# Turning the query and key sets of the mix on VectorE and through DRAM instead of on TensorE

## The reference, cut to what matters

```python
aq, ak, av, bq, bk, bv, cq, ck, cv, cg, gates = split(h @ w_in[l], ...)
qa = rope(rms(aq) * a_q_norm)       # 4 heads x 2 maps x 64
ka = rope(rms(ak) * a_k_norm)
y_a = diff_attention(qa, ka, va, lam, lam_init, a_subln)      # softmax map 1 - lam * softmax map 2
y_b = chunk_attention(rms(bq)*b_q_norm, rms(bk)*b_k_norm, vb, rel_bias)     # 8 heads x 64
y_c = retention(rope(cq), rope(ck) / 8, vc, cg, out_norm)     # 4 heads x 64, decay in place of softmax
x = x + (sum over a, b, c of sigmoid(gates) * (y @ w_branch)) @ w_out
```

## Time and profile before

| | |
|---|---|
| time, median of 3 runs | 1818.6 us (1818.33 to 1820.05) |
| span of the profiled execution, first to last instruction | 1816.7 us |
| the median less this span | 1.9 us |
| busy share: TensorE, its weight loads, VectorE, ScalarE, GpSimd | 99%, 82%, 52%, 50%, 75% |
| granted TensorE clock, mean | 0.999 of full speed |
| DMA | 366.61 MB, 202 GB/s over the span |

### The profile page before, as it was taken

One profiled execution on the slowest core, in us unless ns is written; L12 is line 12 of the kernel. 1 busy time (PEld: TensorE's weight loads), 2 busy tenths in 40 slices (PEclk: granted clock), 3 DMA queues, 4 the chain that ended last, 5 costly groups with the idle time before them and its releaser, 6 DMA issues.

```text
span 1816.7 us, 25068 instructions
## 1 busy us (share of the span) xinstructions
PE 1797.5 (99%) x9322; PEld 1482.3 (82%) x9322; DVE 942.8 (52%) x1756; ACT 905.1 (50%) x1337; POOL 1365.0 (75%) x568
## 2 busy tenths in 40 slices
PE   6999999999999999999999999999999999999999
PEld 5888888887889888887888888888888878888887
DVE  4673766678655524776553230714095865143152
ACT  3334424764456644455554644464445565545442
POOL 2624544559868898987689798969897858888885
PEclk9999999999999999999999999999999999999999
DMA  9853885748775775565466566567655645656653
GB/s 366 299 201 93 278 301 164 196 157 301 245 279 188 221 216 194 172 209 165 132 187 195 175 195 195 193 184 232 195 195 181 186 139 163 194 160 211 190 194 128
DMA packets 200697, 366.61 MB, mean 202 GB/s; under 512 B 32868, under 2 KB 54356, under 8 KB 200020
## 3 DMA queue, kind: packets, MB, share of 16 engines
q1 hardware_dynamic: 197568, 357.39, 61.6%
q10 hardware_dynamic: 3028, 7.86, 1.1%
HBM read 364.12 MB, written 6.13 MB: 204 GB/s over the span
## 4 chain that ended last, share of the span: by engine, by line
PE 98%; DMA 0%; ACTq 0%; ACT 0%; DVE 0%; POOL 0%; issue 0%; DVEq 0%
PE ps L1258 26%; PE ps L1260 26%; PE ps L1259 26%; PE ps L1384 3%; PE ps L1385 3%; PE ps L1386 3%; PE ps L1949 1%; PE ps L1951 1%; PE ps L1950 1%; PE ps L1306 1%; PE ps L1876 1%; PE ps L1655 1%; PE ps L1626 1%; PE ps L1636 1%; PE ps L1516 1%; PE ps L1921 1%
## 5 line engine op out<-in xcount | busy, mean ns | idle before, releaser
L616 POOL TENSOR_TENSOR w_lo<-raw,w_hi 128x1024 fp32r<-128x1024 f32 x556 | 1346.0, 2458 | 403.4 <-ACT w_hi L654 382.2
L1258 PE MATMUL ps<-w_hi,act_rows_r 128*128 128x512 f32 x2064 | 814.8, 395 | 3.2 <-POOL w_lo L616 3.1
L1260 PE MATMUL ps<-w_hi,act_rows_r 128*128 128x512 f32 x2064 | 804.8, 390 | 0.0
L1259 PE MATMUL ps<-w_lo,act_rows_r 128*128 128x512 f32 x2064 | 804.5, 390 | 0.0
L654 ACT ACTIVATE w_hi<-raw 128x1024 fp32r<-128x1024 f32 x556 | 571.1, 1058 | 359.4 <-DMA raw<-in_ffn_w_up 96.5
L1258 PEld LDWEIGHTS ps<-w_hi,act_rows_r 128*128 128x128 f32 x2064 | 387.9, 188 | 89.9 <-issue 8.6
L1260 PEld LDWEIGHTS ps<-w_hi,act_rows_r 128*128 128x128 f32 x2064 | 387.8, 188 | 81.8
L1259 PEld LDWEIGHTS ps<-w_lo,act_rows_r 128*128 128x128 f32 x2064 | 388.1, 188 | 77.2
L2604 DVE STREAM_TRANSPOSE ps<-proj 32x256 f32<-32x256 f32 (+1 forms) x384 | 166.6, 434 | 6.5
L2585 DVE TENSOR_TENSOR proj<-proj,ps 128x1024 f32<-128x1024 f32 (+1 forms) x18 | 20.4, 1132 | 252.2 <-PE ps L1260 247.8
L1384 PE MATMUL ps<-act_rows_r,w_hi 128*128 128x512 f32 (+1 forms) x288 | 101.4, 352 | 0.0
(11 more groups left out here) (245 smaller groups left out, 1559.9 us busy)
## 6 DMA issues: line engine op xcount, KB each, us to landing
raw<-in_w_in SPq DMA_DIRECT2D x120, 512.0 KB, 3.8
raw<-in_ffn_w_gate SPq DMA_DIRECT2D x88, 512.0 KB, 4.3
raw<-in_ffn_w_up SPq DMA_DIRECT2D x88, 512.0 KB, 4.3
raw<-in_ffn_w_down SPq DMA_DIRECT2D x88, 512.0 KB, 3.4
proj<-in_ada_w SPq DMA_DIRECT2D x39, 512.0 KB, 7.8
pt<-in_ada_w SPq DMA_DIRECT2D x38, 512.0 KB, 6.4
raw<-in_pool_w_in SPq DMA_DIRECT2D x32, 512.0 KB, 7.4
raw<-in_na_w_in SPq DMA_DIRECT2D x32, 512.0 KB, 5.4
```

The costliest lines, as they stand in the source:

```text
L616: pool.tensor_tensor(w_lo[:, s, :], raw[:, s, :], w_hi[:, s, :].bitcast(F32), ALU.subtract).then_inc(lo_done, 1)
L1258: pe.matmul(o, h, hi, start=start, stop=False)
L1259: pe.matmul(o, h, lo, start=False, stop=False)
L1260: return pe.matmul(o, c, hi, start=False, stop=stop)
```

## The change

All five sets (AK, AQ, BK, BQ, and CQ with CK) take one way. `set_squared` lets VectorE turn 32 x 32 squares in place of the partition quarter, with two transposes of 128 partitions x 512, one for each 128 tokens, into a staging area of 1024 columns in `proj`. This leaves features on partitions, but only within a quarter: what belongs to partition quarter k lies in the free range k of all four quarters. `keep_set` stores the staging area to a DRAM tensor (`set_rows`, 512 KB, two of them in turn), and `place_set` loads it back in four DMAs, one for each partition quarter, with runs of 1 KB. Both stand in the SyncE queue, behind the sends of block at + 8 and at + 9 of the mix, `at` being the third number in `MIX_SETS`. The staging area is free for the next set when the store has landed.

In `qt` a key set of branch A or B lies in runs of 32 tokens. A query set, and all of the C set, is interleaved: token p of a chunk and tile is at 8 p plus a small offset. So TensorE's stationary operand in every `scores` has a step of 8 words (32 bytes), its moving operand has runs of 32 words for units 0 to 7 and a step of 8 words for units 8 and 9. The number of products, their sizes and their order stay.

The factor 1/8 of AQ moves into the root of the head norms, the gains of BQ into one VectorE multiplication of 128 x 1024 (`queries_scaled`, after block 23, before `maps_joined(3)`). The outputs of branch A and B swap their chunks in `MIX_Y`. The TensorE transposes and the copies from PSUM go, with their waits.

```diff
-MIX_TURNS = ((AK, 4), (AK + 256, 6), (AQ, 0), (AQ + 256, 2), (BK, 12), (BK + 256, 14), (BQ, 8), (BQ + 256, 10), (CK, 18), (CQ, 16))
-MIX_TURN_AT = {13: (2, 3), 19: (6, 7), 31: (8, 9)}
+MIX_SETS = ((AK, 4, 7), (AQ, 0, 10), (BK, 12, 13), (BQ, 8, 18), (CQ, 16, 29))
+            def keep_set(l, q):
+                n = len(MIX_SETS) * l + q
+                sp.wait_ge(dve_done, dve_s.count(("set", l, q)))
+                if n >= 2:
+                    set_landed(sp, l if q >= 2 else l - 1, q - 2 if q >= 2 else q + len(MIX_SETS) - 2)
+                sp.dma_start(set_rows[n % 2], set_blocks([[1, 1024]])).then_inc(sets_kept, 16)
+            def place_set(l, q):
+                n = len(MIX_SETS) * l + q
+                sp.wait_ge(sets_kept, 16 * (n + 1))
+                for kq in range(4):
+                    src = bass.AP(set_rows.tensor, n % 2 * P * 1024 + 256 * kq, [[1024, 32], [32 * 1024, 4], [1, 256]])
+                    sp.dma_start(free(qt[32 * kq:32 * kq + 32, MIX_SETS[q][1], 0:1], [[256, 4], [1, 256]]), src).then_inc(sets_in[n % 2], 16)
...
+                            for q, (_, _, at) in enumerate(MIX_SETS):
+                                if g == at + SLOTS:
+                                    keep_set(layer, q)
+                                if g == at + SLOTS + 1:
+                                    place_set(layer, q)
...
+        def still_heads(chunk, rows, t):
+            base = chunk // 4 * 4
+            return free(qt[rows, base, 0:1], [[8, P]], 2 * (chunk - base) + t)
+        def moving_heads(chunk, rows, t, n):
+            return free(qt[rows, base, 0:1], [[32, n], [256, 4], [1, 32]], 32 * (2 * (chunk - base) + t))
+        def moving_between(chunk, rows, t, n):
+            return free(qt[rows, base, 0:1], [[1, n], [8, P]], 2 * (chunk - base) + t)
...
-                    for k in MIX_TURN_AT.get(G, ()):
-                        turn_heads(k)
...
+                def set_squared(q):
+                    if len(MIX_SETS) * l + q:
+                        dve.wait_ge(sets_kept, 16 * (len(MIX_SETS) * l + q))
+                    for t in range(NT):
+                        rows = free(proj[:, 0:1], [[P, 4], [32, 4], [1, 32]], MIX_SETS[q][0] + t * IN_COLS)
+                        if q in (SET_AK, SET_BK):
+                            last = dve.transpose(set_blocks([[64, 4], [256, 4], [1, 32]], 32 * t), rows)
+                        else:
+                            last = dve.transpose(set_blocks([[2, 4], [256, 4], [8, 32]], t), rows)
...
+                    for q in {0: (SET_AK, SET_AQ), 4: (SET_BK,), 8: (SET_C,)}.get(i, ()):
+                        set_landed(pe, l, q)
+                    if i == 4:
+                        pe.wait_ge(dve_done, dve_s.count(("bq", l)))
...
                             rotated(MIX_ROPED, plain_rope)
                             added(MIX_ROPED, ("rows", l, 2))
+                            dve.wait_ge(dve_done, dve_s.count(("rows", l, 2)))
+                            set_squared(SET_C)
```

More of the change, by code:

```diff
@@ L169, in program @@
     rel_rows = nc.dram_tensor("rel_rows", (LAYERS, P, REL_PITCH), F32, kind="Internal").ap()
+    set_rows = nc.dram_tensor("set_rows", (2, P, 1024), F32, kind="Internal").ap()
     gate_scratch = nc.dram_tensor("gate_scratch", (DEPTH, KC, 2, P), F32, kind="Internal").ap()
@@ L447, in load_bias, with narrow @@
                                       (hp % 2) * 1024 + h * 512 + t * 256), src).then_inc(bias_in[hp % 2], 16)
-            def narrow(w, blocks, nw, stage=None, prev=None, order=None):
+            def keep_set(l, q):
[5 more added lines that the diff above has]
+            def place_set(l, q):
+                n = len(MIX_SETS) * l + q
+                sp.wait_ge(sets_kept, 16 * (n + 1))
+                for kq in range(4):
+                    src = bass.AP(set_rows.tensor, n % 2 * P * 1024 + 256 * kq, [[1024, 32], [32 * 1024, 4], [1, 256]])
+                    sp.dma_start(free(qt[32 * kq:32 * kq + 32, MIX_SETS[q][1], 0:1], [[256, 4], [1, 256]]), src).then_inc(sets_in[n % 2], 16)
+            def narrow(w, blocks, nw, stage=None, prev=None, order=None, layer=None):
                 v = w.rearrange("(c p) n -> p c n", p=P)
@@ L479, in narrow @@
                             ada_weights(a)
+                        if layer is not None:
+                            for q, (_, _, at) in enumerate(MIX_SETS):
[3 more added lines that the diff above has]
+                                    place_set(layer, q)
                     return
@@ L590, in _ @@
                 ffn_weights(I["ffn1_w_gate_2"][l], I["ffn1_w_up_2"][l], I["ffn1_w_down_2"][l], tables=True)
-                narrow(I["w_in_2"][l], 15, 512, f"mix_in{l}", order=MIX_ORDER)
+                narrow(I["w_in_2"][l], 15, 512, f"mix_in{l}", order=MIX_ORDER, layer=l)
                 for j in range(6):
@@ L1042, in root @@
                     c = MIX_STAT[n]
+                    if n == 1:
+                        act.activation(rstat[:, c:c + 16], stat[:, c:c + 16], ACT.Sqrt,
+                                       bias=eps_64[:]).then_inc(act_done, act_s.one(("hrms", l, n)))
+                        return
                     act.activation(rstat[:, c:c + 16], stat[:, c:c + 16], ACT.Sqrt, bias=eps[:],
                                    scale=1.0 / HD).then_inc(act_done, act_s.one(("hrms", l, n)))
[L1046 to L1051, removed]
                 def evicted(n, how):
@@ L1113, in mix @@
                     if G == 20:
-                        act.wait_ge(dve_done, dve_s.count(("keys", l, BK)))
+                        act.wait_ge(dve_done, dve_s.count(("set", l, SET_BK)))
                         for h in range(4):
@@ L1867, in scores @@
                         q, keys = (i, 4 + i) if i < 4 else (4 + i, 8 + i)
-                        parts = ((0, slice(0, P), slice(0, P)), (SEQ, slice(P, SEQ), slice(0, SEQ)))
+                        parts = ((0, 0, 0, 1), (SEQ, 1, 0, 2))
                     else:
                         q, keys = 10 + i, 8 + i
-                        parts = ((0, slice(0, P), slice(0, SEQ)), (SEQ, slice(P, SEQ), slice(P, SEQ)))
-                    for o, still, moving in parts:
+                        parts = ((0, 0, 0, 2), (SEQ, 1, 1, 1))
+                    heads = moving_heads if i < MIX_SOFT else moving_between
+                    for o, still, first, n in parts:
                         for c in range(2):
                             rows = slice(c * HD, (c + 1) * HD)
-                            n = moving.stop - moving.start
-                            last = pe.matmul(ps[:, 4 + c, o:o + n], qt[rows, q, still], qt[rows, keys, moving], start=True, stop=True)
+                            last = pe.matmul(ps[:, 4 + c, o:o + n * P], still_heads(q, rows, still), heads(keys, rows, first, n),
+                                             start=True, stop=True)
                     last.then_inc(pe_done, pe_s.one(("as", l, i)))
@@ L2012, in _ @@
         def _(dve):
+            dve.memset(eps_64[:], HD * EPS)
             dve.memset(eps[:], EPS).then_inc(acc_free[0], 1)
@@ L2691, in inverse @@
                     dve.reciprocal(rstat[:, c:c + 16], rstat[:, c:c + 16]).then_inc(dve_done, dve_s.one(("hrinv", l, n)))
[L2693 to L2697, removed]
+                def set_squared(q):
[7 more added lines that the diff above has]
+                            last = dve.transpose(set_blocks([[2, 4], [256, 4], [8, 32]], t), rows)
+                    last.then_inc(dve_done, dve_s.one(("set", l, q)))
                 def head_rstd(n):
@@ L2712, in mix @@
                 dve.tensor_tensor(k, k, head_rstd(0), ALU.mult).then_inc(dve_done, dve_s.one(("rows", l, 0)))
+                dve.wait_ge(dve_done, dve_s.count(("rows", l, 0)))
+                set_squared(SET_AK)
                 dve.wait_ge(act_done, act_s.count(("hsq", l, 1)))
@@ L2718, in mix @@
                 inverse(1)
-                dve.wait_ge(dve_done, dve_s.count(("rows", l, 0)))
-                keys_turned(AK, 4)
+                dve.wait_ge(dve_done, dve_s.count(("rows", l, 1)))
+                set_squared(SET_AQ)
                 squares(2)
@@ L2823, in probabilities, with queries_scaled @@
                     dve.tensor_copy(pt[:, (i % 2) * 768 + 384:(i % 2) * 768 + 768], ps[:, 7, 0:384]).then_inc(dve_done, dve_s.one(("apt1", l, i)))
[L2825 to L2830, removed]
+                def queries_scaled():
+                    set_landed(dve, l, SET_BQ)
+                    q = free(qt[:, 8, 0:1], [[1, 1024]])
+                    dve.tensor_scalar(q, q, mix_cols[:, 7:8], None, ALU.mult).then_inc(dve_done, dve_s.one(("bq", l)))
                 def y_low(br):
@@ L2886, in mix @@
                         dve.wait_ge(dve_done, dve_s.count(("hrinv", l, 3)))
-                    for k in MIX_TURN_AT.get(G, ()):
-                        turned(k)
+                    if G == 23:
+                        queries_scaled()
                     if i < 4:
```

31 lines of the change are left out of this document (13 added, 18 removed).

## The result

The changed kernel takes 1825.07 us (median of 5 runs, 1824.58 to 1827.46) against 1818.6: the ratio is 1.0035, 95% interval 1.0022 to 1.0047. It is 6.5 us slower. The profiled execution has a span of 1822.8 us, 6.1 more than before.

What follows compares the result with a forecast made beforehand. TensorE was taken to bound the kernel: -5.3 us for removed turns, 2 x 0.3 and 2 x 0.2 us for added waits, -4.3 in sum, so 1818.6 became 1814.3 us; 8-in-10 range 1813.0 to 1823.0.

Steps and rivals of the forecast that it cites:

- the one on the products: At scores on TensorE: reading operands with a step of 8 words costs nothing over the 1.08 us of one scores.
- these far ends: Cost of the stepped queries at scores: nothing at the low end, 1.4 us for each scores (27 us in all) at the high.
- The first rival: At scores, stepped weight loads run at half pace: 6.2 to 8.3 us added, 1820.5 to 1822.6 us; chance 0.36.
- the 2 us that it allowed for stepped writes: Addition to the half-pace case if VectorE's stepped writes of the C set cost twice.
- The turns taken off TensorE: Transposes behind blocks 13, 19 and 31 go: 0.93, 0.86 and 0.86 us, 2.65 a mix, 5.3 for two.
- A transpose in runs: On VectorE, a 128 x 512 transpose estimated at 0.72 us, 1.44 us for a set of two.
- The stepped write: VectorE transposes writing with a step of 8 words: at worst each column costs twice, another 0.53 us per transpose.
- The wait at values(5): TensorE waits for VectorE's copy behind the C set: 0.3 us a mix, 1.4 if stepped writes cost twice.
- BQ's multiplication: VectorE multiplies BQ's gains in 0.75 us, with some 3.2 us of cover before scores(4); costed at nothing.
- The way through DRAM: Store 3.3 us, whole way 7.7 (5.7 to 9.9); four sets covered, C set adds 0.2 us a mix at scores(8).
- the second rival: C set late: waits of 2.2 us at scores(8) and 1.4 at values(5), overlapping; 1818.3 us, no change; chance 0.10.
- The hold of SyncE: Weight sends wait behind stores on the SyncE queue; 18 us of slack left, so costed at nothing.

Runs made afterwards that it cites:

- e1: Changed kernel with the stationary operand of every scores read from 128 words side by side instead of a step of 8: 1821.68 us.
- e3: Kernel before, with only the stationary operand of scores read at a step of 8, 4 or 2 words: 1826.98, 1825.74 and 1819.45 us.
- v4: Changed kernel with all turns in runs of 32, AQ and BQ tokens put side by side by ScalarE and VectorE, C set left to TensorE: 1815.32 us.
- v2: Changed kernel with queries of all sets and C's keys at a step of 2, four sorting stores and one 512 KB load a set: 1867.68 us.
- v1: Changed kernel with A and B queries at a step of 2, four sorting stores and one load a set, C set turned on TensorE: 1855.89 us.
- e4: Changed kernel with the C set turned on VectorE behind the copy for values(5) instead of ahead of it: 1826.82 us.

## Why the prediction was wrong

The forecast was 1814.3 us, the time 1825.07; it lies above the range too.

**The step that failed** is the one on the products: "Between these far ends I take the low one, by the row that it is nearest to: the runs of 32, where leaving words out costs nothing." Runs of 32 are not near a step of 8. They leave out whole stretches and use every word of the 16 bytes they touch; a step of 8 uses one of four. Taken as 0, it is 4.89 us for a mix, 9.8 for both, and that alone turns -4.3 into a loss. The first rival named the mechanism and its place, and its 0.33 us for a unit of A or B was 0.39 to 0.43; for C it gave 0.22 to 0.76, and 0.82 came. Most of that is the step in the keys, the moving operand, which the forecast did not cost either: 0.69 by itself (e1), the queries' step 0.29 by itself (e3). Its price of 6.2 to 8.3 us was too low by 1.5 at its upper end, and its 1820.5 to 1822.6 with it; with the 2 us that it allowed for stepped writes it ended at 1824.6, 0.5 short of the time.

The Trainium skill (Advanced Engine Details and Errata, Memory Cachelines) says that at least two hits on an SBUF line of 16 bytes are needed to absorb the latency. The three steps agree: 192 ns with two words to a line, 321 and 326 with one. The Trainium skill (SBUF — State Buffer, the note on cachelines under Door 1: The DMA port swizzle) adds that one can stride for free as far as 4 fp32 words; here a step of 4 costs 321 ns against 186, so read as a step that is free, that figure does not hold for the stationary operand.

**The turns taken off TensorE** were right: 0.93, 0.87 and 0.86 against 0.93, 0.86 and 0.86.

**VectorE.** A transpose in runs takes 0.69 us (0.72 estimated). The stepped write takes 1.16, near the upper of the two ends (1.25), in 12 of the 20. The wait at values(5) is 0.53 instead of 0.3, and 1.0 in e1: the slow scores(7) hides half of what the stepped writes cost. BQ's multiplication takes 2.05 instead of 0.75 and is covered, within its 3.2 us of cover; why a row of the same size takes a third of it was not tried.

**The way through DRAM** was right for the C set (store 2.9 for 3.3, the way 7.1 and 7.8 for 7.7) and wrong for the other four. Their stores took 5.2 to 8.7 us, about twice the 3.3, and BQ's set landed 17 us after its store was issued, where the upper end was 9.9. The row of a store that the 3.3 rests on, 2.0 us, stands at the very end of the kernel (1806 to 1812 us), where the DMA engines were busy for 0.29 of the time (1810 to 1817 us). They stayed covered, as predicted, but not because the way was as short as it said: that is luck in part, for BQ's set landed only 1.6 us (mix 1: 1.3) before its multiplication began. Around the slow stores the DMA engines were busy for 0.75 to 1.00 of the time, around the C set's for 0.55 and 0.72; that this is the cause was not tested. The prediction also has no term for VectorE, which has one staging area and waits for each store before it turns the next set.

e1 shows what that is worth without the slow scores: mix 0 has then waits of 1.19 (blocks 19 and 20), 1.01 (values(5)) and 1.23 us (scores(8)), mix 1 0.99 and 0.73. Against 2.65 us of turns that leaves +0.8 and -0.9, so with a step that costs nothing in any operand of TensorE, and VectorE's stepped writes and the DMAs as in that one execution, the kernel would have stood, by this estimate, at about 1818.5: no change, the second rival's time, though by waits in three places and not at scores(8) alone. So the forecast lacked a second thing beside the step: the time of the stores and loads beside the weights, and VectorE's wait for them.

**The hold of SyncE** is free in a mix as predicted: no wait of TensorE for GpSimd's w_lo is among its waits in mix 0 or mix 1.

## What to carry to other kernels

Ask of every operand that a new layout touches how many words of each 16 bytes it uses, on TensorE's stationary side above all, where little covered a load here; if the layout must be interleaved, let an engine with idle time put the words side by side, as v4 does, before TensorE reads them. When work is taken off the bound engine, recompute the arrival of everything it waits for on its new, earlier times: a loss that is repaired may uncover a wait that it hid, as values(5) shows. Take the time of a store or a load from a row with the same traffic beside it: stores of one size took 2.9 to 8.7 us in one kernel here. Changing the form of a DMA, by shorter runs or by one transfer for four, can be the dearest part of all.

## What the runs showed that was not expected

- A step of 4 words costs a weight load of 64 x 128 as much as a step of 8 (321 and 326 ns), a step of 2 almost nothing (192 against 186).
- VectorE's transpose pays for a write step of 8 words (1161 against 691 ns), not for a step of 2 (692 in v2).
- Four stores of 128 KB in runs of 256 bytes held the SyncE queue for 9.57 us (AQ's set in v1) and for 2.80 us (AK's).
- One load of 512 KB in place of four of 128 KB let scores(8) begin 10.4 us after its issue (v2); with the four it began 4.7 us after the first, without a wait.
- The same store of 512 KB landed after 2.9 us in one place of the mix and after 5.2 to 8.7 in four others.
- After a wait of 2.05 us in e4 TensorE's granted clock fell to 0.50 for about 3 us and cost 1.6 us more; after 1.16 us in e1 it stayed at 1.00 in the windows that follow.
